# Recurrence of a two-block kernel: the inverse's blocks get products of their own, the other scores are masked between its levels

## What is computed

```python
def wkv7_scan(r, decay, k, v, kk, a, reverse):
    ...
    def step(S, inp):
        r_t, w_t, k_t, v_t, kk_t, a_t = inp
        s_kk = jnp.einsum('bhij,bhj->bhi', S, kk_t)
        S = (S * w_t[:, :, None, :]
             - s_kk[..., None] * (a_t * kk_t)[:, :, None, :]
             + v_t[..., None] * k_t[:, :, None, :])
        return S, jnp.einsum('bhij,bhj->bhi', S, r_t)
...
    wkv = (wkv7_scan(r4, heads(decay(w0_f, wf_lo, w_up_f)), k_f, v4, kk, heads(a_f), False)
           + wkv7_scan(r4, heads(decay(w0_b, wb_lo, w_up_b)), k_b, v4, kk, heads(a_b), True))
```

## Time and profile before

| | us |
|---|---|
| median of 3 runs | 1921.92 |
| lowest and highest | 1921.37 and 1922.57 |
| span of the profiled execution | 1919.5 |
| PE busy in it | 1721.4 |
| DVE busy in it | 919.7 |

### The profile page before, as it was taken

How to read it: one execution, slowest core, us unless ns; L and a number is a source line. 1 busy time by engine, 2 the same in 40 slices (tenths; PEclk the granted TensorE clock), 3 DMA queues, 4 the chain that set the end, 5 groups by cost and what they waited for, 6 DMA issues and landing times.

```text
span 1919.5 us, 30187 instructions
## 1 busy us (share of the span) xinstructions
PE 1721.4 (90%) x12376; PEld 1377.1 (72%) x12376; DVE 919.7 (48%) x1856; ACT 307.1 (16%) x689; POOL 165.6 (9%) x159
## 2 busy tenths in 40 slices
PE   8999999999999999999999999999999765655656
PEld 3888889999888988689999998877778221221214
DVE  4766667897886366734675236644432000000001
ACT  2200000011210012422111114322323000000001
POOL 3000000000133310001000002611001000000000
PEclk9999999999999999999999999989999987787878
DMA  9333333765853113126545863101379999999997
GB/s 374 142 131 130 130 131 132 260 215 191 321 187 110 67 67 132 67 88 220 204 167 194 290 209 119 46 24 57 121 290 368 415 434 428 433 430 434 428 436 303
DMA packets 47336, 428.23 MB, mean 223 GB/s; under 512 B 5395, under 2 KB 6004, under 8 KB 16124
## 3 DMA queue, kind: packets, MB, share of 16 engines
q1 hardware_dynamic: 37584, 389.07, 52.3%
q10 hardware_dynamic: 9644, 37.59, 5.6%
HBM read 425.59 MB, written 1.05 MB: 222 GB/s over the span
## 4 chain that ended last, share of the span: by engine, by line
PE 70%; DMA 19%; DVE 6%; issue 2%; ACT 2%; POOL 1%; SPq 0%; POOLq 0%; DVEq 0%; ACTq 0%
DMA arena<-experts_ring_dram 18%; PE bank L1068 18%; PE bank L1202 14%; PE bank L1252 8%; PE bank L1298 6%; PE bank L1683 3%; PE bank L1398 3%; PE bank L1396 3%; PE bank L1752 2%; PE bank L2057 2%; PE bank L1576 1%; ACT arena L2361 1%; DVE arena L3483 1%; DVE tiny L3285 1%; PE bank L1451 1%
## 5 line engine op out<-in xcount | busy, mean ns | idle before, releaser
L1068 PE MATMUL bank<-arena 128*128 128x128 f32 (+1 forms) x2208 | 355.7, 323 | 0.5 <-ACT arena L2578 0.5
L1068 PEld LDWEIGHTS bank<-arena 128*128 128x128 f32 x2208 | 325.5, 192 | 28.4 <-issue 1.8
L2057 PE MATMUL bank<-arena 128*32 128x512 f32 x1400 | 213.3, 764 | 145.5 <-DMA arena<-experts_ring_dram 145.5
L2057 PEld LDWEIGHTS bank<-arena 128*32 128x32 f32 x1400 | 58.0, 136 | 294.0 <-issue 293.9
L1202 PE MATMUL bank<-arena 128*128 128x256 f32 x880 | 193.9, 379 | 0.0
L1202 PEld LDWEIGHTS bank<-arena 128*128 128x128 f32 x880 | 167.1, 190 | 23.1 <-issue 0.5
L1252 PE MATMUL bank<-arena 128*128 128x128 f32 x1456 | 162.9, 275 | 0.0
L1252 PEld LDWEIGHTS bank<-arena 128*128 128x128 f32 x1456 | 162.8, 192 | 0.1
L3677 DVE TENSOR_TENSOR arena<-arena,bank 128x512 f32<-128x512 f32 x8 | 5.5, 688 | 240.7 <-PE bank L2057 240.7
L1298 PE MATMUL bank<-arena 128*128 128x128 f32 x880 | 102.7, 275 | 0.0
L1298 PEld LDWEIGHTS bank<-arena 128*128 128x128 f32 x880 | 100.7, 192 | 0.2
(11 more groups left out here) (526 smaller groups left out, 2438.1 us busy)
## 6 DMA issues: line engine op xcount, KB each, us to landing
arena<-dense_dram SPq DMA_DIRECT2D x169, 1024.0 KB, 4.9
arena<-experts_ring_dram SPq DMA_DIRECT2D x41, 4096.0 KB, 26.9
arena<-ada_rest_dram ACTq DMA_DIRECT2D x56, 512.0 KB, 4.2
arena<-experts_dram SPq DMA_DIRECT2D x18, 1024.0 KB, 8.8
arena<-ada_head_dram SPq DMA_DIRECT2D x8, 1024.0 KB, 23.5
arena<-experts_dram SPq DMA_DIRECT2D x10, 512.0 KB, 9.4
arena<-tokens_dram ACTq DMA_DIRECT2D x1, 2048.0 KB, 20.4
arena<-experts_ring_dram SPq DMA_DIRECT2D x1, 2048.0 KB, 24.2
```

Source lines behind the costliest of these rows:

```text
L1068: ins = mm(out, lhsT=w, rhs=rhs(k), start=k == 0, stop=k == k_tiles - 1)
L2057: ins = mm(ps[banks[half]][32 * e:32 * e + 32, :], lhsT=lhs[:, 2 * kp + par, CAP * e:CAP * e + CAP], rhs=slab[e][par][:, half * 512:half * ...
```

## The change

- **Own products.** New function `own_products(s)`: B.Q's two diagonal blocks of 64 x 64 per direction and head (32 products of 64x64) and the far block (16 more) are computed by themselves into banks `BQ_AT`, unmasked. New function `own_blocks(s)` on ACT copies them to `AD[s]` and `FB[s]`. POOL's level masks cut `AD[s]` as before. Chunk 0's stand on PE behind V's transposes and ahead of the attention's values; chunk 1's stand in chunk 0, between the far block's two products.
- **Other scores in pairs.** New functions `pair_products(s, p)` and `pair_masked(s, p)`: six pairs of banks 2 and 6 in a chunk, 0 to 3 with KT against Q and R (4 products of 256 columns), 4 and 5 with BT against R (8 products of 128 columns). Pair 0 stands ahead of level 1, pair n behind level n. B.Q no longer goes through `AM`, which shrinks from 4 to 3 blocks a head.
- **First inverse.** DVE makes it ahead of the masking in chunk 0; chunk 1's is made in chunk 0's tail.
- **Wanted values** now stand behind the levels.
- **Keys.** DVE forms Q ahead of KT; `Eneg`, `Einc`, `Eexc` are on other pages. The keys' transposes stand together behind the attention's values.
- **POOL.** `rkk` and the zeroing of pages 19 and 20 no longer wait for the keys. They follow right behind the key scaling. Page 21 is zeroed behind level 1's part.

The core of the diff:

```diff
+BQ_AT = {(0, 0): ((0, 0), (1, 0)), (0, 1): ((3, 0), (7, 0)), (1, 0): ((5, 0), (6, 0)), (1, 1): ((0, 0), (3, 0))}
+FILL_BANKS = (2, 6)
+U_BANKS = (6, 3)
+WV_BANKS = (((0,), (3,)), ((0, 7), (3, 5)))
...
-        AM = page(19, 8192, 512)
+        AM = page(19, 16 * 384, 384)
...
-            pool.wait_ge(keys_ready, 1)
+            for t in range(US_R, US_R + 4):
+                evacuated(pool, "shift", *shift_at(t))
+            pool.wait_ge(kd_ready, 2)
+            nc.gpsimd.tensor_tensor(rkk, kd256[:, 0:4, :], kd256[:, 4:8, :], add).then_inc(rk_step, 1)
             nc.gpsimd.memset(page(19, 2048), 0.0).then_inc(am_zero, 1)
-            pool.wait_ge(keys_ready, 2)
-            nc.gpsimd.memset(page(21, 4096), 0.0).then_inc(am_zero, 1)
-            pool.wait_ge(keys_ready, 3)
-            nc.gpsimd.memset(page(20, 2048), 0.0).then_inc(am_zero, 1)
-            nc.gpsimd.tensor_tensor(rkk, kd256[:, 0:4, :], kd256[:, 4:8, :], add).then_inc(rk_step, 1)
             pool.wait_ge(rk_step, 1)
             for j in range(4):
                 nc.gpsimd.tensor_scalar(rkk[:, j, :], rkk[:, j, :], c("rk", j), None, mult).then_inc(rk_step, 1)
+            nc.gpsimd.memset(page(20, 2048), 0.0).then_inc(am_zero, 1)
             pool.wait_ge(rk_step, 5)
             nc.gpsimd.tensor_tensor(rkk, rkk, US[:, US_R:US_R + 4, :], mult).then_inc(rk_step, 1)
...
+            def own_products(s):
+                for d in range(2):
+                    for par in range(2):
+                        take(pe, f"bq{s}", *BQ_AT[s, d][par])
+                    ch = d if s == 0 else 1 - d
+                    for j in range(4):
+                        row = 8 * d + 2 * j + ch
+                        for par, q_ in ((0, 0), (1, 1), (0, 1), (1, 0)):
+                            b, r64, o64 = BQ_AT[s, d][par][0], slice(H * par, H * par + H), slice(H * q_, H * q_ + H)
+                            ins = mm(ps[b][o64, H * j:H * j + H], lhsT=BT[r64, row, o64], rhs=QQ[r64, 2 * row, o64],
+                                     start=True, stop=True)
...
             pe.wait_ge(keys_ready, 1)
-            keys_to_tokens(0)
+            own_products(0)
...
+            pe.wait_ge(keys_ready, 2)
+            keys_to_tokens(0)
             keys_to_tokens(1)
...
+            def pair_products(s, p):
+
+                d = p // 2 if p < 4 else p - 4
+                ch = d if s == 0 else 1 - d
+                for b in FILL_BANKS:
+                    take(pe, f"am{s}", b, p)
...
+                pair_products(s, 0)
                 for lv in range(1, N_LEV):
...
+                    pair_products(s, lv)
+
+                wanted_values(s)
...
+                if s == 0:
+                    own_products(1)
+                else:
+                    gate2(2, 0, 4)
...
+            def own_blocks(s):
...
+                for d in range(2):
+                    for par in range(2):
+                        b, use = BQ_AT[s, d][par]
+                        got(act, f"bq{s}", b, use)
+                        ins = A(heads_of(AD[s][:, 8 * d:8 * d + 8, :], par), ps[b][:, 0:T].rearrange("p (j n) -> p j n", n=H), ACT.Copy)
...
+            do(tt_(QQv[:, 0:8, 0, :], kkn, Eexc[:, 0:8, :], mult))
+            settle()
+            tt_(QQv[:, 8:16, 0, :], kkn, Eexc[:, 8:16, :], mult).then_inc(keys_ready, 1)
             dve.wait_ge(kd_ready, 2)
...
+            def pair_masked(s, p):
...
+                for par, b in enumerate(FILL_BANKS):
+                    got(dve, f"am{s}", b, p)
+                    rows = AM[:, 8 * d:8 * d + 8, :].rearrange("p (j r) n -> p j r n", r=2)
+                    if p < 4:
+                        j = 2 * (p % 2)
+                        V.copy_predicated(rows[:, j:j + 2, par, 0:T], keep_bits[:, d, :].rearrange("p (j n) -> p j n", n=T),
+                                          ps[b][:, :].rearrange("p (j n) -> p j n", n=T)).then_inc(evac[b], 1)
...
+            first_inverse(0)
+            for s in range(2):
+                pair_masked(s, 0)
...
+                if s == 0:
+                    first_inverse(1)
```

More of the change, by code:

```diff
@@ L1687, in gate2 @@
                     ins.then_inc(full[b], 1)
-            for s in range(2):
-                for d in range(2):
-                    ch = d if s == 0 else 1 - d
-                    for j in range(4):
-                        row = 8 * d + 2 * j + ch
-                        for half, keys in enumerate((BT, KT)):
-                            for par in range(2):
-                                b, r0 = 2 * (j % 2) + par, 64 * par
-                                if half == 0:
-                                    take(pe, f"am{s}", b, 2 * d + j // 2)
-                                ins = mm(ps[b][:, half * T:half * T + T], lhsT=keys[r0:r0 + 64, row, :],
-                                         rhs=QQw[r0:r0 + 64, row, :], start=True, stop=True)
-                                if half:
-                                    ins.then_inc(full[b], 1)
-                lo64, hi64 = slice(0, H), slice(H, P)
+            lo64, hi64 = slice(0, H), slice(H, P)
@@ new lines, in pair_products @@
+            def pair_products(s, p):
[3 more added lines that the diff above has]
+                    take(pe, f"am{s}", b, p)
+                for j in range(2 * (p % 2), 2 * (p % 2) + 2) if p < 4 else range(4):
+                    row = 8 * d + 2 * j + ch
+                    for par, r64 in enumerate((lo64, hi64)):
+                        b = FILL_BANKS[par]
+                        if p < 4:
+                            o = j % 2 * T
+                            ins = mm(ps[b][:, o:o + T], lhsT=KT[r64, row, :], rhs=QQw[r64, row, :], start=True, stop=True)
+                            last = j % 2 == 1
+                        else:
+                            ins = mm(ps[b][:, j * P:j * P + P], lhsT=BT[r64, row, :], rhs=QQ[r64, 2 * row + 1, :], start=True, stop=True)
+                            last = j == 3
+                        if last:
+                            ins.then_inc(full[b], 1)
@@ new lines, in wanted_values @@
+                                ins.then_inc(full[b], 1)
+                    return
+                evacuated(pe, "tail0", 1, 0)
+                evacuated(pe, "tail0", 6, 1)
+                for d in range(2):
+                    for b in WV_BANKS[1][d]:
+                        take(pe, "wv1", b, 0)
+                    for j in range(4):
+                        for par in range(2):
+                            hd = 2 * j + par
+                            mm(ps[WV_BANKS[1][d][par]][:, 64 * j:64 * j + 64], lhsT=AM[:, 8 * d + hd, AM_KQ:AM_KQ + P],
+                               rhs=Vtok[:, 1 - d, 64 * hd:64 * hd + 64], start=True, stop=False)
+                        row = 8 * d + 2 * j + 1 - d
+                        for par, r64 in enumerate((lo64, hi64)):
+                            b = WV_BANKS[1][d][par]
+                            ins = mm(ps[b][:, 64 * j:64 * j + 64], lhsT=QQ[r64, 2 * row, :], rhs=state_v[r64, d, j, :],
+                                     start=False, stop=True)
+                            if j == 3:
+                                ins.then_inc(full[b], 1)
@@ L1773, in _ @@
                         diagonal(ps[bx], d, XT, Pw).then_inc(full[bx], 1)
+                    pair_products(s, lv)
+                wanted_values(s)
+                for par in range(2):
+                    evacuated(pe, f"bq{s}", *BQ_AT[s, 1][par])
                 for d in range(2):
                     evacuated(pe, f"inv{s}", (1, 5)[d], 4)
-                    take(pe, f"inv{s}", 3 * d, 5)
+                take(pe, f"far{s}", 1, 0)
                 for hd in range(HEADS):
```

229 lines of the change are left out of this document (111 added, 118 removed).

## The result

The changed kernel takes **1909.3 us** (median of 4 runs, 1908.77 to 1912.8); the kernel before, on the same chip, 1921.64 (4 runs). The ratio estimated from all runs is 0.9942, 95% interval 0.9927 to 0.9956: faster by 0.6% (the two medians alone give 0.9936).

A forecast was written before the change was run, and what follows sets the result against it. PE's row of work up to the recurrence's end was taken to set the start of the expert loads; terms gave -15.5, then +6.9 for POOL's moved work, -8.6 in all: 1913.4 us median, range 1906.5 to 1919.

The forecast's parts named there:

- likeliest case: Whole kernel: the forecast's own sum of -8.6 us holds, giving 1911 to 1916 us; chance 0.53.
- POOL yields: POOL's moved work beside DVE: POOL yields or few turns are lost, -11 to -15.5, 1906.4 to 1911 us; chance 0.20.
- The signs named: Changed profile: own products near 1212 behind a DVE-ended pause of some 5 us, level 1 near 1224.5, levels of 5.0.
- pairs: PE's scores, 19.7 us, are replaced by six pairs of trace products per chunk, 5.8 each chunk, twice 11.6.
- own products: PE, both chunks: 96 trace products of 64x64 each, 3.2 us with starts, twice 6.4, all on PE's path.
- pauses of before that go: PE's idle time ahead of level 1, ahead of L1736, behind last levels and in seven levels disappears: 9.3 us.
- half clock that goes: PE's half-clock losses behind the earlier pauses disappear: 1.3 + 1.0 in L1752, 3.7 in L1736 and L1742, together 6.0 us.
- new waits: Behind the start: ACT's table load and sigmoid 0.5, bank 6 for chunk 1's pair 0 0.75, second gate 0.3; together 1.6.
- Q late by `rkk`: PE's pause: Ahead of chunk 0's own products: POOL's moved work delays DVE by 6.9 us, Q comes at 1212.6, PE waits 5.2.
- half clock behind it: Chunk 0's own products: the clock falls behind PE's wait for Q, costing 1.7 us.
- The clock rival: Chunk 1: thin L1736 and L1742 pull the clock down without a pause; -3.2 to -6, 1915.9 to 1918.7 us; chance 0.14.

The follow-up runs named there:

- the repeat: The changed kernel run once more, unaltered: 1910.66 us (6 runs), ratio 0.9943 to the kernel before.
- the base: The changed kernel itself, which all follow-up runs edit: 1909.3 us, ratio 0.9942 to the kernel before.
- two quadrants: The changed kernel with its 64x64 own products reordered so that two quadrants of PE's array alternate in place of four: 1911.35 us, ratio 0.9944 to the kernel before.

## Why the prediction was right, and where it was wrong

The median is 4.1 below the forecast of 1913.4 and inside the wide range of 1906.5 to 1919. It is outside the 1911 to 1916 of the likeliest case, and so is the repeat with 1910.66; both lie where the rival "POOL yields" (chance 0.20) had put them. The signs named are there, but the own products of chunk 0 start near 1209.6 (1211.1 in the repeat) and not 1212, and level 1 near 1220.4 and not 1224.5. The sum of the steps was -8.6 at the end of the recurrence, measured are -10.3, of which 0.5 is an earlier start. That it is so close is in good part luck: errors of several us met with opposite signs.

| step | forecast | measured |
|---|---|---|
| pairs | +11.6 | +12.9: 8 at 1.07, 4 at 1.09 |
| own products | +6.4 | +3.2 at full clock: 1.56 and 1.65 |
| pauses of before that go | -9.3 | gone, all of them |
| a level's last product ends under the next pair | not counted | about -1.8: 3.88 a level in place of 4.06 |
| half clock that goes | -6.0 | 2.3 went; the wanted values are at 10.0 (6.4 forecast), the rows behind lose 2.2 |
| new waits | +1.6 | +1.95: 0.25, 0.78, 0.62, and 0.47 - 0.17 |
| Q late by `rkk`: PE's pause | +5.2 | +2.57 and 2.81 |
| half clock behind it | +1.7 | +1.2, and 0 in the repeat |

In the kernel before, a wait stood at V's transposes that no term counted and that went as well:

```profile
1207.88 1.06 PE L1652 MATMUL bank<-small,arena 128*128 128x128 f32 x8 [0.40 <-ACT arena L2493]
```

With the measured terms and this one the forecast would be -8.6 + 1.3 - 3.2 - 1.8 + 5.8 + 0.3 - 2.6 - 0.5 - 0.4 = -9.7 (in the table's order, the 5.8 being 6.0 less 2.3 and 0.1, plus the 2.2 behind), against -9.8 without the earlier start.

- **The structure held.** Scores out, pairs under the levels, PE as the bound of a level (4.94, forecast 5.0) with DVE 0.8 to spare (forecast 0.95), chunk 1 within 2 us of chunk 0's tail (first pair at 1267.51), and the stream of loads moving with it.
- **The clock rival came true.** It had a chance of 0.14 and "-3.2 to -6" as its result, which did not come, because own products, levels and Q cost less than forecast. The step that failed is the half clock that goes: 3.7 for L1736 and L1742 was counted as a consequence of the pause of 1.45 ahead of them. The base shows the fall without any pause, in both profiles, and the gates between them take it away. The granted clock falls while these products run, with PE busy. Part of the 10.0 is no clock: the new order changes between L1776 and L1781 after four in place of eight, and a step of four and four costs 0.96 at full clock, so eight steps are 7.7, where the forecast took 6.4 from eights in the earlier trace rows.
- **Q's lateness was mis-sized.** The mechanism was right: POOL's work beside DVE's, PE's pause ended by Q. The forecast charged DVE with 6.9 of POOL's 8.4; it lost 4.2. The four TENSOR_SCALARs (3.63) cost 0.4 and not nearly their own time, so the rival "POOL yields" was half right too: it holds for them, and not for the sum (2.1) and the product (2.0). The row that said so was L3420, cited in the prediction against the rule and then not followed.
- **Own products.** The forecast took L1752's pace for the same shape; the rows gave half of it.
- **New waits.** The forecast put 0.5 on ACT's table load. It was bank 6, read out by ACT's token copies, and that was 0.78.

## What to carry to other kernels

When a change moves one engine's work beside another's, price each operation by its kind and by who yields, from a row where the two ran together. A step at half clock that follows a pause need not come from the pause: the clock fell here under thin work with the engine busy throughout, and mixing it with wide work that had to be done anyway took that away at the price of one wait of 0.51. When a step of a sum is small beside its neighbours' uncertainty, a total that comes out near says little about the steps.

## What the runs showed of the hardware that was not expected

- The granted clock fell to 0.50 under the wanted values (64 columns, 120 ns a product) with no idle time ahead: at about 1298 in the base, inside a stage that is busy throughout, in all seven profiles with that stage unbroken, for about 10 us in six of them and 6.6 in one. With a 256-column product behind every second or each pair it stayed at 1.00 in all four that had them. Under the levels (64 columns too, 30 ns a product) it was 1.00.
- Pauses of PE of 2.57 (base) and 2.98 (two quadrants) ahead of chunk 0's own products were followed by 0.50; pauses at the same place of 2.81 (the repeat, and the run with the own products not hidden), 2.83 and 3.00 (the runs with gates in between) were not. The length of such a pause alone did not tell whether the clock would fall.
- POOL's TENSOR_SCALARs beside DVE's two-input products gave way (7.65 to 8.08 for four, 3.63 alone beside masked copies), while POOL's two-input operations held DVE up by 2.0 and 2.1, a little under their own 2.36 (3.25 against 1.22, 6.00 against 3.89). DVE lost 0.4 to all four TENSOR_SCALARs.
- Products of 64x64 ran at 15 ns each where four quadrants took turns, at 19 with two, and at 30 in the levels (two quadrants, one bank).
